# Stick-breaking stage: the gate's Exp and Ln one projection piece later, its product behind the taps, and the diagonal mask as an fp32r product

## The chip, the cores and the metric

One core of a Trainium2 chip runs the whole program in one launch. The metric is the device time of one execution in microseconds (us). The engines are named as the profile names them: PE (matrix engine), PEld (its weight loads), DVE (vector), ACT (scalar), POOL (GpSimd) and SP (the engine that issues most DMAs).

## The reference

A sequence of 1024 tokens with 1024 features goes through two blocks. The first (a gated MLP with spatial mixing, then a dilated window attention) is not touched. The second block projects each token and mixes with three groups of heads. These parts of it matter here:

```python
def stick_breaking_attention(q, k, v, valid):
    ...
        z = jnp.einsum('bhqd,bhkd->bhqk', q[:, :, start:end], k[:, :, :end]).astype(jnp.float32) * scale
        mask = (pos[None, :end] < pos[start:end, None]) & valid[None, :end]
        log_keep = jnp.where(mask, jax.nn.log_sigmoid(-z), 0.0)
        csum = jnp.cumsum(log_keep, axis=-1)
        log_w = jax.nn.log_sigmoid(z) + (csum[..., -1:] - csum)
        w = jnp.where(mask, jnp.exp(jnp.where(mask, log_w, 0.0)), 0.0)
    ...
    xbc = jax.nn.silu(causal_depthwise_conv(jnp.concatenate([xs, bm, cm], axis=-1) * vmask, conv_w, conv_b))
    ...
    y = y.reshape(bsz, L, SSD_W) * jax.nn.silu(z.astype(f32))
```

A query sees only the keys before it, so the blocks on the diagonal of the score matrix are masked. The projection's units xs, bm and cm go through a convolution of four taps and a silu; the units z, q and g of the other groups go through a silu alone. The kernel computes silu(y) as y * exp(-ln(1 + exp(-y))).

## The kernel before, in words

The stage is `projection_and_sticks` (L2492). It runs from about 2050 to 2600 us of the execution. Several things are interleaved in it by hand, and each engine follows the order that `drive` (L2585) writes out.

*The projection.* 27 units of 128 output features are computed for 1040 tokens. Each unit u has three pieces (j = 0, 1, 2: 352, 344 and 344 tokens). On PE a piece is 24 products of fp32r operands (L155: for each of 8 groups of features, three combinations of upper and lower halves). The weights of a unit are split beforehand into an upper half by ACT (L137, called by `w.split_hi` in piece j = 1 of the unit before) and a lower half by DVE (L142, `w.split_lo`, also in piece j = 1). DVE evicts each piece with a multiplication (`evict`, L2996) once PE has finished it. SP loads the weights two units ahead.

*The gates.* Units 7 to 14 go through the convolution (`is_x`), units 15 to 22 through the silu alone (`is_silu`). For a convolution unit v, DVE runs taps 0 and 1 in piece (v+1, 0) (L3074, L3076), and taps 2 and 3 (L3080, two instructions) and a clamp into the tile `ce` (L3083) in piece (v+1, 1). For a silu unit it runs a clamp alone in piece (v+1, 1) (L3089). ACT runs Exp (L2742) in piece (v+1, 1), then Ln (L2745) and Exp (L2747) in piece (v+1, 2), all on `ce`. DVE multiplies in piece (v+2, 0) (`finish`, L3011), and SP stores the unit in piece (v+2, 1).

*The sticks.* There are 56 slots (4 heads by 14 blocks of 128 keys with up to 512 queries). In slot c PE computes the scores of slot c+1 (L2918, fp32 operands), on the diagonal adds the mask by a product of the identity with a constant of 0 and -1e30 (L2921, fp32 operands), then adds the running sums to the scores of slot c (L2931: two products with a matrix of -1, where earlier blocks exist; L2933: two products with a triangle of -1), then runs the values of slot c-1 (L2902), then a share of a piece. ACT runs Abs, Exp and Ln (L2767, L2769, L2771) on the scores of c+1, the Exp of slot c (L2777), and the upper halves of the accumulator and of the sticks (L2780, L2786). DVE runs the accumulator (L3101, L3103), the softplus (L3112), and the lower halves (L3117, L3121). PE writes the next scores into a bank only once L2777 has read it, and waits before L2931 and L2933 for the lower halves.

*The state-space chunks.* Behind the sticks, phases of the chunked recurrence (class `Ssd`, L2274) take the place of the slots. Among them, L2342 on PE reads `ab`, which DVE copies in L2409; L2387 on ACT reads what the transposes of L2348 wrote, and PE's L2354 overwrites that bank.

Pieces 15 to 59 lie in the slots, at most one ends in a slot; the later ones lie between the phases. On each engine the instructions of a slot or phase stand ahead of those of its piece, and a waiting instruction holds up all behind it. All synchronisation is by semaphores. The constants come from `constants` (L3978); ACT copies the triangle and the matrix of -1 into fp32r tiles at the stage's start (L2711, L2712).

Of the kernel before, what the change touches and what calls it, by code (L numbers as in the profile page):

```python
# [16 lines left out]
F32R = mybir.dt.float32r  # L17
ACT = mybir.ActivationFunctionType
# [3 lines left out]
P = 128  # L22
# [4 lines left out]
HALF = 512  # L27
# [2457 lines left out]
def stick_tiles(nc):  # L2485

    with Stage(nc, "hs") as st:
        heads = st.sb("heads", [P, 4, LM])
        return heads, (st.sb("acc_lo", [P, HALF], F32R), st.sb("tri", [P, P], F32R), st.sb("ones", [P, P], F32R))


def projection_and_sticks(nc, a, w, hi, lo, inv, x, x_again, x_out, over_x, heads, hg, keep, table, cst, proj, conv, o_cat, ident, ones):  # L2492
# [10 lines left out]
    NU = len(units)  # L2503
# [16 lines left out]
    k_groups = lambda c: range(KT * rest * c // N, KT * rest * (c + 1) // N) if 0 <= c < N else ()  # L2520
    in_slot = lambda c: [first_slot + x // KT for x in k_groups(c) if x % KT == KT - 1]
    tok = lambda kt: (0, META) if kt == 0 else (META + (kt - 1) * P, P)
    neg_tri, neg_ones, neg, blocks = (cst[n] for n in ("neg_suffix", "neg_ones", "not_before", "block64"))
    with Stage(nc, "pr") as st:
        heads, (acc_lo, tri_r, ones_r) = heads
        qn, kn = ([heads[:, 2 * b + i, :] for i in range(2)] for b in range(2))
        vt, rows, sd_tile, sticks = over_x
        dtf, tmp, af = (rows[n] for n in ("dtf", "tmp", "af"))
# [166 lines left out]
        def _(act):  # L2695
# [13 lines left out]
            act.wait_ge(s_par, 16 * 7)  # L2709
            act.wait_ge(s_table, 16)  # L2710
            nc.scalar.activation(tri_r[:, :], neg_tri, ACT.Copy)  # L2711
            nc.scalar.activation(ones_r[:, :], neg_ones, ACT.Copy).then_inc(s_tri, 1)  # L2712
            for u in (2,):
                w.split_hi(act, u % 2, u // 2, free=(s_mm, 3 * (u - 2) + 3))
# [6 lines left out]
            def piece(p):  # L2721
                u, j = p // 3, p % 3
                if j == 0 and u - 3 in qk:
                    root(u - 3)
                if j == 1 and u + 1 < NU:
                    w.split_hi(act, (u + 1) % 2, (u + 1) // 2, free=(s_mm, 3 * (u - 1) + 3))
                if u - 2 in qk:
                    i = qk.index(u - 2)
                    if j == 0:
                        act.wait_ge(s_ev, 3 * (u - 2) + 3)  # L2730
                        wait(act, s_blk, 3 * i)
                        nc.scalar.activation(ce[:, :], ev[(u - 2) % 3][:, TAPS - 1:], ACT.Square).then_inc(s_psq, 1)
                    c0, c1 = PIECES[j]
                    act.wait_ge(s_blk, 3 * i + j + 1)
                    if j == 0:
                        wait(act, s_nrm, i - 1)
                    nc.scalar.activation(cy[i % 2][:, c0:c1], pb[:, 0:c1 - c0], ACT.Ln, bias=eps[:, :], scale=1.0 / HD).then_inc(s_pb, 1)
                if gated(u - 1):
                    n = n_gated(u - 1)
                    if j == 1:  # L2740
                        act.wait_ge(s_cm, n + 1)
                        nc.scalar.activation(ce[:, :], ce[:, :], ACT.Exp, scale=-1.0).then_inc(s_cx, 1)  # L2742
                    if j == 2:
                        act.wait_ge(s_cx, n + 1)
                        nc.scalar.activation(ce[:, :], ce[:, :], ACT.Ln, bias=1.0).then_inc(s_cl, 1)  # L2745
                        act.wait_ge(s_cl, n + 1)
                        nc.scalar.activation(ce[:, :], ce[:, :], ACT.Exp, scale=-1.0).then_inc(s_ce, 1)  # L2747
                if (u, j) == (DT + 2, 0):
                    act.wait_ge(s_sdp, 64)
                    nc.scalar.activation(par[:, 2:3], par[:, 1:2], ACT.Exp).then_inc(s_dte, 1)  # L2750
                    act.wait_ge(s_dt, 2)
                    nc.scalar.activation(tmp, tmp, ACT.Exp, scale=-1.0).then_inc(s_dte, 1)
                    act.wait_ge(s_dte, 2)
                    nc.scalar.activation(tmp, tmp, ACT.Ln, bias=1.0).then_inc(s_dte, 1)
                if (u, j) == (DT + 4, 0):
                    act.wait_ge(s_dtc, 5)
                    for name in ("ecum", "wend", "elast"):
                        nc.scalar.activation(keep[name], keep["cum" if name == "ecum" else name], ACT.Exp).then_inc(s_dtx, 1)
# [75 lines left out]
        def _(pe):  # L2834
# [71 lines left out]
            def slot(c):  # L2906
                if c + 1 < N:
                    h, (qb, kt, q0, n, diag) = (c + 1) // NS, steps[(c + 1) % NS]
                    hs = slice((h % 2) * HD, (h % 2 + 1) * HD)
                    k0, mp = tok(kt)  # L2910
                    b = (c + 1) % 2
                    if (c + 1) % NS == 0:
                        pe.wait_ge(s_nrm, 2 * (h // 2) + 2)
                    if c < 1:
                        pe.wait_ge(s_ev, 6)
                        pe.wait_ge(s_tri, 1)
                    wait(pe, s_w, c)
                    last = nc.tensor.matmul(zb[b][0:mp, 0:n], kn[h // 2][hs, k0:k0 + mp], qn[h // 2][hs, META + q0:META + q0 + n],  # L2918
                                            start=True, stop=False, skip_group_check=True)
                    if diag:  # L2920
                        last = nc.tensor.matmul(zb[b][0:mp, 0:P], ident, neg, start=False, stop=False, skip_group_check=True)  # L2921
                    last.then_inc(s_z, 1)
                if 0 <= c < N:
                    qb, kt, q0, n, diag = steps[c % NS]
# [26 lines left out]
        def _(dve):  # L2951
# [60 lines left out]

            def piece(p):
                u, j = p // 3, p % 3
                if j == 1 and u + 1 < NU:
                    w.split_lo(dve, (u + 1) % 2, (u + 1) // 2)
                if j == 0 and u - 3 in qk:
                    i = qk.index(u - 3)
                    dve.wait_ge(s_scaled, 1)
# [2 lines left out]
                                                   cy[i % 2][:, :], ALU.mult, ALU.mult).then_inc(s_nrm, 1)  # L3022
                    dve.wait_ge(s_nrm, i + 1)
                evict(u, j)
                if (u, j) == (DT + 1, 1):
                    dve.wait_ge(s_kept, 16 * KT)
                    dve.wait_ge(s_sdp, 64)
                    dve.wait_ge(s_ev, 3 * u)
                    nc.vector.memset(dtf[:, 0:P - META], 0.0)
                    nc.vector.memset(tmp[:, 0:P - META], 0.0)  # L3030
                    nc.vector.tensor_scalar(dtf[:, P - META:], ev[DT % 3][0:SSD_HEADS, TAPS - 1:], par[:, 0:1], None, ALU.add).then_inc(s_dt, 1)
                    dve.wait_ge(s_dt, 1)
                    nc.vector.scalar_tensor_tensor(tmp[:, P - META:], dtf[:, P - META:], -1.0, dtf[:, P - META:], ALU.mult, ALU.max).then_inc(s_dt, 1)
# [17 lines left out]
                if u - 2 in vs:  # L3051
# [10 lines left out]
                            nc.vector.tensor_copy(vt[i][:, 4:8, :], src).then_inc(s_pb, 1)  # L3062
                    else:
                        nc.vector.tensor_copy(vt[i][:, 8, :], pb[:, 0:P]).then_inc(s_pb, 1)
                if j == 0 and gated(u - 2):
                    finish(u - 2)
                if is_x(u - 1):
                    v, n = u - 1, n_gated(u - 1)
                    src = ev[v % 3]
# [7 lines left out]
                    if j == 1:  # L3077
# [3 lines left out]
                        dve.wait_ge(s_cc, 4 * n + 4)  # L3081
                        wait(dve, s_out, n)
                        nc.vector.tensor_scalar(ce[:, :], y, LOWEST, None, ALU.max).then_inc(s_cm, 1)  # L3083
                if is_silu(u - 1) and j == 1:
                    v, n = u - 1, n_gated(u - 1)
                    wait(dve, s_gone[v % 2], 16 * (n // 2))
# [891 lines left out]
def constants():  # L3978
# [3 lines left out]
        "ones": (i >= 0) & (j >= 0),  # L3982
        "neg_suffix": np.where(i >= j, -1, 0),
        "neg_ones": np.full((P, P), -1),
        "not_before": np.where(i < j, 0, -1e30),
        "block64": i // 64 == j // 64,
        "upto": i <= j,
        "levels": np.concatenate([(i // B == j // B) & (i % B < B // 2) & (j % B >= B // 2)
# [161 lines left out]
```

## Time and profile before

| what | us |
| --- | --- |
| median of three runs | 3622.37 |
| lowest and highest run | 3618.87, 3626.86 |
| the profiled execution, its own time | 3614.36 |
| its span in the trace | 3612.6 |
| PE busy in the span | 3451.5 (96%) |
| DVE busy | 2170.2 (60%) |
| ACT busy | 1537.2 (43%) |
| mean granted clock of PE, share of full speed | 0.978 |

Times in a row are microseconds from the start of the span. A row of the order of time gives start, duration, engine, line, operation, output and inputs, their shapes, the count of merged instructions, and in brackets how long the engine was idle before it and what ended that. A matmul's duration includes its passage through the array; how fast PE moves on is seen from the start of the next row. PEclk is the granted clock as a share of 2.4 GHz.

### The profile page before, as it was taken

What the parts mean: (1) busy time and instruction counts of PE and PEld (TensorE: products, weight loads), DVE (VectorE), ACT (ScalarE), POOL (GpSimd) and SP (SyncE); (2) the same over time, 40 slices, a digit from 0 to 9 for tenths busy, and PEclk for the clock granted to TensorE, in tenths of its full rate; (3) what the DMA queues carried; (4) which work ended last, traced back from release to release, by engine and by line L of the source; (5) the groups of instructions that cost most, each with busy time, mean ns of one, the idle gap of its engine ahead of it and who ended that gap; (6) DMA issues with size and microseconds to landing.
All of it is one profiled execution on the core that took longest, in us unless ns stands there. A gap on an engine that the chain in (4) does not pass through costs nothing. (4 is left out here: it accounts for less than half of the span.)

```text
span 3612.6 us, 48153 instructions
## 1 busy us (share of the span) xinstructions
PE 3451.5 (96%) x17578; PEld 2817.6 (78%) x17578; DVE 2170.2 (60%) x4264; ACT 1537.2 (43%) x3062; POOL 121.9 (3%) x151
## 2 busy tenths in 40 slices
PE   8999999989999999999999799999879989999999
PEld 6878887867777777777777687778867877878887
DVE  5477773575555666666675646656666566644443
ACT  4254453445444454544444445555224322232222
POOL 0000001000000000000000200000000000000000
PEclk9999999999999999999999999999989999999999
DMA  4232225622111221222233300112232222322223
GB/s 147 94 106 92 88 91 187 193 68 62 59 59 55 65 66 63 68 65 64 67 100 123 124 28 32 50 56 77 96 108 91 96 86 72 108 93 94 99 94 123
DMA packets 162585, 316.84 MB, mean 88 GB/s; under 512 B 33744, under 2 KB 79360, under 8 KB 162224
## 3 DMA queue, kind: packets, MB, share of 16 engines
q1 hardware_dynamic: 144432, 268.49, 22.5%
q0 software_dynamic: 15808, 36.89, 3.3%
q10 hardware_dynamic: 2112, 8.39, 0.6%
q8 instruction: 142, 2.33, 0.3%
q14 instruction: 91, 0.75, 0.1%
HBM read 260.22 MB, written 59.71 MB: 89 GB/s over the span
## 5 line engine op out<-in xcount | busy, mean ns | idle before, releaser
L142 DVE TENSOR_TENSOR all_w_lo<-all_w_raw,all_w_hi 128x1024 fp32r<-128x1024 f32 x241 | 295.1, 1225 | 256.8 <-ACT all_w_hi L137 256.8
L137 ACT ACTIVATE all_w_hi<-all_w_raw 128x1024 fp32r<-128x1024 f32 x241 | 253.5, 1053 | 454.8 <-PE om_z L155 261.5
L155 PE MATMUL om_z<-all_hi,all_w_hi 128*128 128x512 f32 x640 | 256.9, 401 | 7.5 <-DVE all_w_lo L142 4.3
L155 PE MATMUL om_z<-all_hi,all_w_lo 128*128 128x512 f32 x640 | 255.1, 399 | 0.0
L155 PE MATMUL om_z<-all_lo,all_w_hi 128*128 128x512 f32 x640 | 253.6, 396 | 0.0
L2122 DVE CUSTOM_DVE_ANT_0 at_logit<-da_qk,at_bias 128x256 f32<-128x256 f32 (+1 forms) x384 | 130.1, 377 | 164.2 <-issue 163.6
L155 PE MATMUL pr_g<-all_hi,all_w_hi 128*128 128x344 f32 (+1 forms) x624 | 217.7, 349 | 11.4 <-PEq L45 4.9
L1668 ACT ACTIVATE at_p<-at_logit,da_pair_max 128x256 f32<-128x256 f32 (+1 forms) x384 | 177.5, 465 | 100.3 <-DVE da_pair_max L2122 100.3
L1660 ACT ACTIVATE at_pt<-da_tr 128x512 f32<-128x512 f32 (+1 forms) x192 | 101.2, 527 | 263.6 <-PE da_tr L1860 263.4
L155 PE MATMUL pr_g<-all_hi,all_w_lo 128*128 128x344 f32 (+1 forms) x624 | 206.4, 331 | 0.0
L155 PE MATMUL pr_g<-all_lo,all_w_hi 128*128 128x344 f32 (+1 forms) x624 | 205.2, 329 | 0.0
L155 PE MATMUL om_z<-om_h_hi,all_w_hi 128*128 128x512 f32 x512 | 202.3, 395 | 1.7 <-DVE all_w_lo L142 1.7
L155 PE MATMUL om_z<-om_h_lo,all_w_hi 128*128 128x512 f32 x512 | 200.1, 391 | 0.0
L155 PE MATMUL om_z<-om_h_hi,all_w_lo 128*128 128x512 f32 x512 | 200.0, 391 | 0.0
L3968 DVE TENSOR_TENSOR all_yo<-all_yo,om_z 128x512 f32<-128x512 f32 x80 | 55.0, 687 | 183.4 <-PE om_z L155 183.3
L1870 PE MATMUL da_pv<-at_v,at_pt 128*128 128x64 f32 x1280 | 164.1, 267 | 0.0
L1870 PEld LDWEIGHTS da_pv<-at_v,at_pt 128*128 128x128 f32 x1280 | 159.8, 192 | 1.9
L2139 DVE TENSOR_TENSOR da_o<-da_pv,da_rden 128x128 f32<-128x128 f32 x192 | 56.0, 292 | 167.4 <-PE da_pv L1870 161.8
L155 PEld LDWEIGHTS om_z<-all_hi,all_w_hi 128*128 128x128 f32 x640 | 121.9, 190 | 36.9 <-DVE all_w_lo L142 4.5
L1196 ACT ACTIVATE all_w_hi<-all_w_raw 128x512 fp32r<-128x512 f32 x190 | 118.3, 623 | 72.4 <-PE da_by L1214 23.8
L3863 ACT ACTIVATE om_h_hi<-om_m 128x512 fp32r<-128x512 f32 x64 | 40.4, 632 | 254.5 <-DVE om_m L3966 254.5
L155 PEld LDWEIGHTS om_z<-all_lo,all_w_hi 128*128 128x128 f32 x640 | 121.6, 190 | 27.8
(827 smaller groups left out, 8908.0 us busy)
## 6 DMA issues: line engine op xcount, KB each, us to landing
all_w_raw<-in_w_mlp SPq DMA_DIRECT2D x128, 512.0 KB, 3.4
all_w_raw<-in_w_qkv SPq DMA_DIRECT2D x136, 256.0 KB, 2.7
all_w_raw<-in_w_ug SPq DMA_DIRECT2D x48, 512.0 KB, 4.1
all_w_raw<-in_w_in SPq DMA_DIRECT2D x27, 512.0 KB, 3.5
all_w_raw<-in_w_v SPq DMA_DIRECT2D x20, 512.0 KB, 4.6
vhat<-ag_vst ACTq DMA_DIRECT2D x4, 2048.0 KB, 7.4
ow_v<-vhat SPq DMA_DIRECT2D x16, 512.0 KB, 3.4
da_before<-o_groups POOLq DMA_DIRECT2D x32, 256.0 KB, 3.9
```

The source lines that it names most:

```text
L137: self.nc.scalar.activation(self.hi[b][:, :], self.raw[b][:, :], ACT.Copy).then_inc(self.hi_done[b], 1)
L142: self.nc.vector.tensor_tensor(self.lo[b][:, :], self.raw[b][:, :], self.hi[b][:, :].bitcast(F32), ALU.subtract).then_inc(self.lo_done[b], 1)
L155: last = self.nc.tensor.matmul(out, wp[b][:, w], ap[:, k, cols], start=(k == 0 and m == 0), stop=(k == KT - 1 and m == 2))
L1196: self.nc.scalar.activation(self.hi[n % self.slots], self.tile[name], ACT.Copy, scale=self.scales[j] if name in ("a11", "a12") else 1.0).t ...
L1660: nc.scalar.activation(pt[t % 2][:, 0:wd], tr[:, 0:wd], ACT.Copy).then_inc(s_pt, 1)
L1668: last = nc.scalar.activation(p[t % 2][:, hh, 0:wd], logit[t % 2][:, hh, 0:wd], ACT.Exp, scale=-1.0, bias=pair_max[:, t, hh:hh + 1], accum ...
L1870: last = nc.tensor.matmul(pv[:, 64 * hh:64 * hh + 64], pt[t % 2][:, i * P:i * P + P], v[:, t + x, 64 * hh:64 * hh + 64], start=(x == 0), s ...
L2122: last = nc.vector.tensor_tensor_reduce(out=logit[t % 2][:, hh, 0:wd], in0=qk[hh][:, 0:wd], in1=bias[ag][hh][x][:, :], scale=1.0, scalar=3 ...
L2139: nc.vector.tensor_tensor(o[:, t, :].rearrange("p (h c) -> p h c", h=2), pv[:, 0:P].rearrange("p (h c) -> p h c", h=2), rden[:, t, :].rear ...
L3863: nc.scalar.activation(h_hi[:, i, :], m[n % 2][:, :], ACT.Square)
L3968: nc.vector.tensor_tensor(x[:, i, halves[h]], x[:, i, halves[h]], z[b][:, :], ALU.add).then_inc(s_ev, 1)
```

## The change

- ACT runs the gate's Exp and Ln together in piece (v+1, 2), and the last Exp in piece (v+2, 0).
- DVE evicts a piece ahead of splitting the lower half of the next weights, and runs `finish` of unit v behind taps 0 and 1 of unit v+1.
- The mask of the diagonal blocks is the product of the fp32r triangle, which was already there, with a new constant `edge` in one more fp32r tile. `edge` has 2^100 in its last row and -2^100 just above the diagonal; under the triangle of -1 the two cancel for a key before the query, and give -2^100 otherwise.

```diff
--- before.py
+++ after.py
@@ -2486,7 +2486,7 @@
 
     with Stage(nc, "hs") as st:
         heads = st.sb("heads", [P, 4, LM])
-        return heads, (st.sb("acc_lo", [P, HALF], F32R), st.sb("tri", [P, P], F32R), st.sb("ones", [P, P], F32R))
+        return heads, (st.sb("acc_lo", [P, HALF], F32R), *(st.sb(n, [P, P], F32R) for n in ("tri", "ones", "edge")))
 
 
 def projection_and_sticks(nc, a, w, hi, lo, inv, x, x_again, x_out, over_x, heads, hg, keep, table, cst, proj, conv, o_cat, ident, ones):
@@ -2520,9 +2520,9 @@
     k_groups = lambda c: range(KT * rest * c // N, KT * rest * (c + 1) // N) if 0 <= c < N else ()
     in_slot = lambda c: [first_slot + x // KT for x in k_groups(c) if x % KT == KT - 1]
     tok = lambda kt: (0, META) if kt == 0 else (META + (kt - 1) * P, P)
-    neg_tri, neg_ones, neg, blocks = (cst[n] for n in ("neg_suffix", "neg_ones", "not_before", "block64"))
+    neg_tri, neg_ones, edge, blocks = (cst[n] for n in ("neg_suffix", "neg_ones", "edge", "block64"))
     with Stage(nc, "pr") as st:
-        heads, (acc_lo, tri_r, ones_r) = heads
+        heads, (acc_lo, tri_r, ones_r, edge_r) = heads
         qn, kn = ([heads[:, 2 * b + i, :] for i in range(2)] for b in range(2))
         vt, rows, sd_tile, sticks = over_x
         dtf, tmp, af = (rows[n] for n in ("dtf", "tmp", "af"))
@@ -2709,6 +2709,7 @@
             act.wait_ge(s_par, 16 * 7)
             act.wait_ge(s_table, 16)
             nc.scalar.activation(tri_r[:, :], neg_tri, ACT.Copy)
+            nc.scalar.activation(edge_r[:, :], edge, ACT.Copy)
             nc.scalar.activation(ones_r[:, :], neg_ones, ACT.Copy).then_inc(s_tri, 1)
             for u in (2,):
                 w.split_hi(act, u % 2, u // 2, free=(s_mm, 3 * (u - 2) + 3))
@@ -2735,16 +2736,16 @@
                     if j == 0:
                         wait(act, s_nrm, i - 1)
                     nc.scalar.activation(cy[i % 2][:, c0:c1], pb[:, 0:c1 - c0], ACT.Ln, bias=eps[:, :], scale=1.0 / HD).then_inc(s_pb, 1)
-                if gated(u - 1):
+                if gated(u - 1) and j == 2:
                     n = n_gated(u - 1)
-                    if j == 1:
-                        act.wait_ge(s_cm, n + 1)
-                        nc.scalar.activation(ce[:, :], ce[:, :], ACT.Exp, scale=-1.0).then_inc(s_cx, 1)
-                    if j == 2:
-                        act.wait_ge(s_cx, n + 1)
-                        nc.scalar.activation(ce[:, :], ce[:, :], ACT.Ln, bias=1.0).then_inc(s_cl, 1)
-                        act.wait_ge(s_cl, n + 1)
-                        nc.scalar.activation(ce[:, :], ce[:, :], ACT.Exp, scale=-1.0).then_inc(s_ce, 1)
+                    act.wait_ge(s_cm, n + 1)
+                    nc.scalar.activation(ce[:, :], ce[:, :], ACT.Exp, scale=-1.0).then_inc(s_cx, 1)
+                    act.wait_ge(s_cx, n + 1)
+                    nc.scalar.activation(ce[:, :], ce[:, :], ACT.Ln, bias=1.0).then_inc(s_cl, 1)
+                if gated(u - 2) and j == 0:
+                    n = n_gated(u - 2)
+                    act.wait_ge(s_cl, n + 1)
+                    nc.scalar.activation(ce[:, :], ce[:, :], ACT.Exp, scale=-1.0).then_inc(s_ce, 1)
                 if (u, j) == (DT + 2, 0):
                     act.wait_ge(s_sdp, 64)
                     nc.scalar.activation(par[:, 2:3], par[:, 1:2], ACT.Exp).then_inc(s_dte, 1)
@@ -2918,7 +2919,7 @@
                     last = nc.tensor.matmul(zb[b][0:mp, 0:n], kn[h // 2][hs, k0:k0 + mp], qn[h // 2][hs, META + q0:META + q0 + n],
                                             start=True, stop=False, skip_group_check=True)
                     if diag:
-                        last = nc.tensor.matmul(zb[b][0:mp, 0:P], ident, neg, start=False, stop=False, skip_group_check=True)
+                        last = nc.tensor.matmul(zb[b][0:mp, 0:P], tri_r[:, :], edge_r[:, :], start=False, stop=False, skip_group_check=True)
                     last.then_inc(s_z, 1)
                 if 0 <= c < N:
                     qb, kt, q0, n, diag = steps[c % NS]
@@ -3012,8 +3013,6 @@
 
             def piece(p):
                 u, j = p // 3, p % 3
-                if j == 1 and u + 1 < NU:
-                    w.split_lo(dve, (u + 1) % 2, (u + 1) // 2)
                 if j == 0 and u - 3 in qk:
                     i = qk.index(u - 3)
                     dve.wait_ge(s_scaled, 1)
@@ -3022,6 +3021,8 @@
                                                    cy[i % 2][:, :], ALU.mult, ALU.mult).then_inc(s_nrm, 1)
                     dve.wait_ge(s_nrm, i + 1)
                 evict(u, j)
+                if j == 1 and u + 1 < NU:
+                    w.split_lo(dve, (u + 1) % 2, (u + 1) // 2)
                 if (u, j) == (DT + 1, 1):
                     dve.wait_ge(s_kept, 16 * KT)
                     dve.wait_ge(s_sdp, 64)
@@ -3062,8 +3063,6 @@
                             nc.vector.tensor_copy(vt[i][:, 4:8, :], src).then_inc(s_pb, 1)
                     else:
                         nc.vector.tensor_copy(vt[i][:, 8, :], pb[:, 0:P]).then_inc(s_pb, 1)
-                if j == 0 and gated(u - 2):
-                    finish(u - 2)
                 if is_x(u - 1):
                     v, n = u - 1, n_gated(u - 1)
                     src = ev[v % 3]
@@ -3081,6 +3080,8 @@
                         dve.wait_ge(s_cc, 4 * n + 4)
                         wait(dve, s_out, n)
                         nc.vector.tensor_scalar(ce[:, :], y, LOWEST, None, ALU.max).then_inc(s_cm, 1)
+                if j == 0 and gated(u - 2):
+                    finish(u - 2)
                 if is_silu(u - 1) and j == 1:
                     v, n = u - 1, n_gated(u - 1)
                     wait(dve, s_gone[v % 2], 16 * (n // 2))
@@ -3982,7 +3983,7 @@
         "ones": (i >= 0) & (j >= 0),
         "neg_suffix": np.where(i >= j, -1, 0),
         "neg_ones": np.full((P, P), -1),
-        "not_before": np.where(i < j, 0, -1e30),
+        "edge": 2.0 ** 100 * ((i == P - 1).astype(int) - (i == j - 1)),
         "block64": i // 64 == j // 64,
         "upto": i <= j,
         "levels": np.concatenate([(i // B == j // B) & (i % B < B // 2) & (j % B >= B // 2)
```

## Rows read from the trace of the kernel before

**Rows 1.** Windows: engines' busy us (instructions), PE's granted clock, DMA share, GB/s.

```profile
2100.00:2200.00 100.00, 96.76 (x540) 79.82 (x539) 54.38 (x101) 53.96 (x105) 0.00 (x0) 0.98 0.09 28
2200.00:2300.00 100.00, 90.15 (x481) 74.02 (x480) 65.36 (x115) 58.35 (x111) 0.00 (x0) 0.91 0.12 40
2300.00:2400.00 100.00, 89.82 (x462) 72.62 (x461) 64.99 (x108) 54.98 (x101) 0.00 (x0) 0.91 0.12 41
```

**Rows 2.** PE's waits, 2100 to 2440: us in total, times, longest.

```profile
PE pr_zb L2918 <- ACT pr_wt L2777: 17.4, 9, 3.7
PE pr_zb L2931 <- DVE ox_sticks L3121: 4.6, 6, 1.5
```

**Rows 3.** The longest waits, same stretch, all engines: one of ACT.

```profile
ACT pr_ce L2742 <- DVE pr_ce L3083: 43.9, 8, 7.5
```

**Rows 4.** Order of time around one stalled slot of the sticks.

```profile
2249.06 1.04 ACT L137 ACTIVATE all_w_hi<-all_w_raw 128x1024 fp32r<-128x1024 f32 x1
...
2249.19 0.69 DVE L3121 TENSOR_TENSOR ox_sticks<-pr_sp,pr_sp_hi 128x512 fp32r<-128x512 f32 x1
...
2249.59 1.12 PE L2918 MATMUL pr_zb<-hs_heads 64*128 64x512 f32 x2
2250.13 1.23 DVE L142 TENSOR_TENSOR all_w_lo<-all_w_raw,all_w_hi 128x1024 fp32r<-128x1024 f32 x1 [0.25 <-ACT all_w_hi L137]
...
2250.64 0.45 PE L2931 MATMUL pr_zb<-ox_sticks,hs_ones 128*128 128x384 f32 x1
...
2251.27 0.51 DVE L2996 TENSOR_TENSOR pr_ev<-pr_g,all_inv 128x344 f32<-128x344 f32 x1
...
2251.70 2.63 DVE L3080 SCALAR_TENSOR_TENSOR pr_cy<-pr_ev,pr_taps,pr_cy 128x1040 f32<-128x1040 f32 x2
...
2254.36 0.70 DVE L3083 TENSOR_SCALAR pr_ce<-pr_cy 128x1040 f32<-128x1040 f32 x1
...
2255.10 1.07 ACT L2742 ACTIVATE pr_ce<-pr_ce 128x1040 f32<-128x1040 f32 x1 [5.00 <-DVE pr_ce L3083]
2255.12 0.55 DVE L3103 TENSOR_TENSOR pr_acc<-pr_acc,pr_sp 128x384 f32<-128x384 f32 x1
...
2258.43 0.69 DVE L3112 SCALAR_TENSOR_TENSOR pr_sp<-pr_zb,pr_e 128x512 f32<-128x512 f32 x1 [2.76 <-ACT pr_e L2771]
...
2258.94 2.07 PE L2918 MATMUL pr_zb<-hs_heads 64*128 64x512 f32 x2 [3.67 <-ACT pr_wt L2777]
...
2260.04 0.69 DVE L3121 TENSOR_TENSOR ox_sticks<-pr_sp,pr_sp_hi 128x512 fp32r<-128x512 f32 x1
```

**Rows 5.** Windows of 5 us, columns as in rows 1.

```profile
2280.00:2285.00 5.00, 2.33 (x9) 1.04 (x8) 2.59 (x4) 4.79 (x10) 0.00 (x0) 1.00 0.00 0
2525.00:2530.00 5.00, 5.00 (x24) 4.97 (x24) 2.26 (x5) 0.83 (x1) 0.00 (x0) 0.70 0.00 0
```

**Rows 6.** Order of time around two stalls in the state-space phases.

```profile
2485.48 0.52 DVE L2996 TENSOR_TENSOR pr_ev<-pr_g,all_inv 128x344 f32<-128x344 f32 x1 [1.21 <-PE pr_g L155]
...
2488.28 1.91 PE L2342 MATMUL pr_ob<-mixers_cst,ox_ab 128*128 128x128 f32 x15 [2.17 <-DVE ox_ab L2409]
...
2519.93 1.22 DVE L142 TENSOR_TENSOR all_w_lo<-all_w_raw,all_w_hi 128x1024 fp32r<-128x1024 f32 x1 [2.69 <-ACT all_w_hi L137]
...
2523.19 0.58 ACT L2387 ACTIVATE pr_sp<-pr_zb 128x512 f32<-128x512 f32 x1
...
2523.83 0.66 PE L2354 MATMUL pr_zb<-all_ident,ox_zf 128*128 128x128 f32 x4 [3.51 <-ACT pr_sp L2387]
```

**Rows 7.** Order of time on PE in one diagonal slot.

```profile
2196.44 0.49 PE L2921 MATMUL pr_zb<-mixers_cst,all_ident 128*128 128x128 f32 x2
...
2196.68 0.31 PE L2933 MATMUL pr_zb<-pr_sp_hi,hs_tri 128*128 128x128 f32 x1
...
2196.82 0.28 PE L2933 MATMUL pr_zb<-ox_sticks,hs_tri 128*128 128x128 f32 x1
```

**Rows 8.** Order of time on ACT near the stage's start.

```profile
2061.37 0.29 ACT L2711 ACTIVATE hs_tri<-mixers_cst 128x128 fp32r<-128x128 f32 x1
```


## The prediction, made before the change was run

> **What bounds the kernel now.** I first read the windows [rows 1], because the change lives in one stage, the second block's projection with the stick-breaking attention in it, from about 2050 to 2600 us. While no gated unit is in it (2100 to 2200) PE is busy 96.76 of 100 us at a granted clock of 0.98. In the next two hundreds it is busy 90.15 and 89.82 us at 0.91. So PE paces the stage, and from 2200 on it loses in two ways: 20 us stand idle, and the busy time is partly at the lower of the clock's two levels, 1.2 instead of 2.4 GHz. At half speed a busy share of 1 - 0.91 in windows with 180 busy us costs 180 x 0.09 = 16.2 us.
>
> Then the list of PE's waits [rows 2]: 17.4 us in 9 waits stand before L2918 (the next slot's scores), which waits for ACT's L2777 (the Exp that makes the attention weights); 4.6 us in 6 waits stand before L2931, which waits for DVE's L3121. The full list says why ACT is late [rows 3]: it stood 43.9 us in 8 waits at L2742, the gate's first Exp, for DVE's L3083, the clamp behind the taps of the convolution.
>
> One such wait in order of time [rows 4] is the case to follow. ACT has split the next weights by 2250.10 and stands at L2742 for 5.00 us: DVE must first split the lower half (L142), evict (L2996), run two taps (L3080) and clamp (L3083), to about 2255.0. Queued behind L2742 on ACT are the next slot's Abs, Exp, Ln and L2777. They finish after 2258.4, so PE, which had ended its work at 2258.94 - 3.67 = 2255.27, stands 3.67 us. Then its L2918 takes 2.07 us where it took 1.12 at 2249.59: the clock has fallen. Windows of 5 us show which stalls do that [rows 5]: from 2280 to 2285 PE is busy 2.33 of 5 us, idle in two stalls of under 2 us, and the clock stays 1.00; behind the stall of 3.51 us [rows 6] it is 0.70. Among the stalls here those of 1.5 us mostly pass, and those above 2 us mostly don't.
>
> **The gate on ACT.** Removed: ACT's wait at piece j = 1. Exp and Ln stand together at j = 2, where the clamp has long been done, since at most one piece falls in a slot; the last Exp stands at the next j = 0. ACT's work per unit is as before (three activations of 1.07 us); j = 2 keeps two, j = 0 takes the one that j = 1 gives up. In that case [rows 4] ACT is then free at 2250.10, its three small activations and L2777 follow the scores that are ready at 2250.64, and L2918 of the next slot finds its weights made. The 17.4 us go, as cause. What is late next is DVE, which still has the clamp ahead of the next slot's chain.
>
> **The order on DVE.** The eviction now comes ahead of L142. In the same case: eviction at 2249.88 (behind the previous L3121), L142 at 2250.31, taps at 2251.45, clamp at 2254.11, accumulator (L3103) at 2254.73, L3112 at about 2255.20. From L3112's start to L3121's end the trace shows 2260.73 - 2258.43 = 2.30 us with ACT's upper half between [rows 4]. So the sticks are ready at 2257.5, and PE wants them at 2255.27 + 1.05 (the scores, 2249.59 to 2250.64) = 2256.3. A stall of 1.2 us is left before L2931, where 3.67 stood. I worked the other seven convolution units in the same way, from their own shapes: 1.35, 0, 0.45, 1.05, 0.2, 0 and 1.1 us; the small ones are slots with short diagonal blocks. All eight: 5.3 us. Three of these hold up to 1.2 us from the swap itself: where L142 used to run while DVE waited for PE's piece, it now stands behind the eviction. For the gates without taps the clamp follows at once and no new stall comes.
>
> Of the 4.6 us before L2931, three waits of 2.0 us together come in the slot right behind one that ACT made late, and belong to the 5.3 now; 2.6 stay (bounds: none or all of the 4.6). Idle saved among the sticks: 17.4 + 2.0 - 5.3 = 14.1 us. The last product (L3011) behind the taps delays only its store; DVE waits there for an Exp that ACT has run before the eviction. SP's stores of the finished units go out about 2.1 us later (the two taps of piece j = 0 now stand ahead of L3011: half of L3080's two a piece), and so do POOL's loads that follow the last of them, whose data PE takes several phases later: nothing; without that cover it would cost 2.1 us twice.
>
> **The clock.** With stalls of 1.35 us at most I expect most of the 16.2 us back, and keep 3.5 for one or two falls: 12.7 us. Bounds: 6 us, if the stalls of 1.0 to 1.5 us fall together with others, and 16.2.
>
> **The diagonal mask.** 32 products (64 records: two for each fp32 product) become fp32r products of one record. At full clock the fp32 one moves PE on by 0.24 us (2196.44 to 2196.68 [rows 7]), an fp32r one of the same 128x128 shape with the same weights by 0.14 (to 2196.82). Saved: 32 x 0.10 = 3.2 us; a little of it lies in slots where DVE ends the wait, so I take 2.9. Bounds: 0 (PE gets no further by it) and 32 x 0.24 = 7.7 (the product costs nothing). The Trainium skill ("FP8 and Floating Point Precision", TensorE Precision Notes) says that true FP32 makes four passes through the array; by that alone the product would fall to a quarter, 0.06 us, and the sum would be 2.6 us better. No quarter is seen here: the trace has 0.14 us against 0.24 [rows 7], and the measurement decides. The copy of the new constant is one ACT instruction of 0.29 us [rows 8], ahead of the split of unit 2, whose DVE half stands behind five evictions: hidden; with that cover gone it costs 0.3.
>
> **Behind the sticks.** Two stalls of the state-space phases are touched [rows 6]. At 2523.83 PE had stood 3.51 us for ACT's L2387, which was queued behind L2742, since ACT had finished its split before L142 started at 2519.93. PE's own transposes, which L2387 reads, were done when its stall began, 2523.83 - 3.51 = 2520.3. Without the wait L2387 starts then instead of at 2523.19: 2.9 us, and the clock's fall behind it (0.70 over 5 us [rows 5]) another 1.5. Against it, at 2485.48 DVE had done L142 while it waited for PE; now L142 stands behind the eviction and ahead of L2409, for which PE already stands 2.17 us: 1.2 us lost. Net 3.2 us.
>
> **Sum.** 14.1 + 12.7 + 2.9 + 3.2 = 32.9 us. The profiled execution took 3614.36 (span 3612.6 and 1.8 around it): 3581.5. It lies 8.0 below the median of the runs, 3622.37, so against the median the change gives 3589.5; I say 3590. Nothing behind the stage is changed, and it moves forward as a whole: its last stretch is a DVE chain that starts from PE's phases.
>
> **Rivals.**
> *DVE takes the wait over (17%).* The swap and the taps hit all twelve gated units among the sticks, not eight: 1.2 us is left at each, 14.4 of 19.4, the clock gives back half (8), the mask 3, the phases 1. Gain 17 us: 3605. For it: DVE was already the releaser of 4.6 us, and its slots get shorter when PE is faster. Against it: gates without taps need 2 us less of DVE.
> *The stall only changes its name (5%).* PE waits as long before L2931 as it did before L2918, the clock falls as often, and the mask alone is left: 3 us, 3619. The order of time [rows 4] speaks against it: the chain from the clamp to the sticks is 2.8 us and starts at the same time as before, but no longer has ACT's Exp of 1.07 and four activations in front.
> *Slower (3%).* The swap's place is L142 between eviction and taps. If the upper halves were ready long before PE's piece ends, each of twelve slots would have 1.2 us more on DVE, 14.6 in all, on top of unchanged stalls, less 3 for the mask: 3634. It decides once ACT's L137 ends over 1.2 us ahead of the piece; in the case above it ends 0.4 us behind it (2250.10 against the end at about 2249.6), and only at 2483.05 is DVE that early.
> *The mask saves nothing* lies inside the forecast: 3593.
>
> **How the numbers follow.** The forecast has 75%. Its own range is 3577 to 3600: no stalls left and the whole clock back is 9 us better, a few us are the scatter of medians (the three runs span 8 us), and on the other side the clock's lower bound. To hold eight in ten with the first rival partly in, the range is 3577 to 3610. A measurement of this kernel tells about 0.2%, 7 us, from no change. Faster (under 3615): 0.75 + 0.17 less 0.01 = 0.91; within: 0.06; slower: 0.03.
>
> **What would show it.** Right: no wait of PE on L2777 between 2196 and 2416 except crumbs; ACT's waits at the gate's Exp for L3083 gone; waits before L2931 for L3121 between 5 and 11 us in all, none above 1.5; the granted clock of these two hundreds at 0.97 or more; the mask's product one record of 128x128 and PE moving on within 0.15 us. The stall before L2354 under 1 us, that before L2342 near 3.4. Wrong: L3121 as releaser of 15 us or more, the clock still near 0.91, or PE waiting for lower halves (L142).

## The result, and the profile after

The changed kernel takes 3584.19 us (median of 4 runs, 3583.30 to 3586.79); the kernel before takes 3624.61 us beside it (4 runs, 3618.87 to 3630.26). The ratio is 0.989 with a 95% interval of 0.9872 to 0.9907: 40 us, or 1.1%, faster. The forecast was 3590, with 3577 to 3610 as its range.

The windows of the middle of the stage, of the kernel after, answer to [rows 1]:

```profile
2100.00:2200.00 100.00, 96.64 (x528) 79.50 (x527) 52.78 (x100) 55.25 (x109) 0.00 (x0) 0.97 0.08 26
2200.00:2300.00 100.00, 97.22 (x558) 79.39 (x557) 78.30 (x137) 68.19 (x127) 0.00 (x0) 1.00 0.13 48
2300.00:2400.00 100.00, 97.51 (x556) 80.29 (x555) 72.07 (x126) 66.74 (x125) 1.85 (x2) 1.00 0.21 68
```

Where gated units run, PE was busy 90 of 100 us at a clock of 0.91; now it is busy 97 at 1.00. The number of its instructions per window rises from 481 to 558: this is the gain. Its waits from 2100 to 2420 us, kernel after, answer to [rows 2]:

```profile
PE pr_zb L2932 <- DVE ox_sticks L3122: 5.2, 5, 1.4
PE pr_pb L2885 <- ACT pr_ce L2733: 2.2, 1, 2.2
PE pr_zb L2934 <- DVE ox_sticks L3122: 1.2, 1, 1.2
```

The 17.4 us before the scores are gone altogether. (Lines have moved: L2932 is L2931 of before, L2934 is L2933, L3122 is L3121, L2919 is L2918, L2922 is L2921, L2778 is L2777, L2997 is L2996, L2885 is L2884, and L3079 and L3082 are L3080 and L3083.) What is left of the sticks' own waits is for their lower half, 5.2 us before L2932 and 1.2 before L2934. The 2.2 us before L2885 were 2.2 in the kernel before too. The slot that the prediction followed [rows 4] looks like this in the order of time, kernel after:

```profile
2243.09 0.51 DVE L2997 TENSOR_TENSOR pr_ev<-pr_g,all_inv 128x344 f32<-128x344 f32 x1
...
2243.51 1.22 DVE L142 TENSOR_TENSOR all_w_lo<-all_w_raw,all_w_hi 128x1024 fp32r<-128x1024 f32 x1
...
2244.65 2.63 DVE L3079 SCALAR_TENSOR_TENSOR pr_cy<-pr_ev,pr_taps,pr_cy 128x1040 f32<-128x1040 f32 x2
...
2245.93 0.59 ACT L2778 ACTIVATE pr_wt<-pr_zb 128x512 f32<-128x512 f32 x1
...
2247.32 0.70 DVE L3082 TENSOR_SCALAR pr_ce<-pr_cy 128x1040 f32<-128x1040 f32 x1
...
2248.54 1.12 PE L2919 MATMUL pr_zb<-hs_heads 64*128 64x512 f32 x2
...
2249.79 1.05 ACT L2742 ACTIVATE pr_ce<-pr_ce 128x1040 f32<-128x1040 f32 x1
2249.93 0.69 DVE L3122 TENSOR_TENSOR ox_sticks<-pr_sp,pr_sp_hi 128x512 fp32r<-128x512 f32 x1
...
2250.67 0.51 PE L2932 MATMUL pr_zb<-ox_sticks,hs_ones 128*128 128x512 f32 x1 [1.01 <-DVE ox_sticks L3122]
```

ACT makes the weights at 2245.93, before DVE even starts the clamp at 2247.32, so PE starts the next scores at 2248.54 without a wait and at full clock (1.12 us, not 2.07). ACT's Exp of the gate (L2742) follows at 2249.79, behind the slot's own work, and no longer waits for the clamp. DVE is late next, by 1.01 us; the prediction had 1.2.

The two stalls behind the sticks, kernel after, in order of time, answer to [rows 6]:

```profile
2451.66 0.52 DVE L2997 TENSOR_TENSOR pr_ev<-pr_g,all_inv 128x344 f32<-128x344 f32 x1 [2.35 <-PE pr_g L155]
...
2452.09 1.22 DVE L142 TENSOR_TENSOR all_w_lo<-all_w_raw,all_w_hi 128x1024 fp32r<-128x1024 f32 x1
...
2455.47 2.83 PE L2342 MATMUL pr_ob<-mixers_cst,ox_ab 128*128 128x128 f32 x12 [3.18 <-DVE ox_ab L2409]
...
2489.28 0.60 ACT L2387 ACTIVATE pr_sp<-pr_zb 128x512 f32<-128x512 f32 x1 [0.46 <-PE pr_zb L2348]
...
2489.93 0.66 PE L2354 MATMUL pr_zb<-all_ident,ox_zf 128*128 128x128 f32 x4 [0.69 <-ACT pr_sp L2387]
```

L2354 waits 0.69 instead of 3.51 us. L2342 waits 3.18 instead of 2.17 us, since DVE, which stood idle for 2.35 us ahead of the eviction, has the split of 1.22 us still to do behind it. And the mask, on PE, kernel after, answers to [rows 7]:

```profile
2115.51 0.33 PE L2922 MATMUL pr_zb<-hs_edge,hs_tri 128*128 128x128 f32 x1
2115.68 0.28 PE L2932 MATMUL pr_zb<-ox_sticks,hs_ones 128*128 128x128 f32 x1
```

One record, and PE moves on after 0.17 us instead of 0.24. The median over the 32 products is 0.164 instead of 0.244 us, so that together they save 2.6 us.

To compare kernels I use two windows of each: from the first to the last scores (the sticks), and from there to the last eviction (behind). What I call the clock's part is the length of a stretch times one minus its granted clock. With the two digits that the windows below show it would be good to 1.8 us only, so I add it up over windows of 5 us, which is good to 0.2. It counts a little too much where PE stands idle at the low clock. Kernel before, then kernel after:

```profile
2106.30:2464.30 358.00, 332.83 (x1788) 271.50 (x1788) 222.06 (x393) 211.94 (x398) 1.84 (x2) 0.95 0.12 42
2464.30:2597.90 133.60, 123.39 (x803) 118.88 (x801) 91.12 (x158) 49.57 (x88) 7.93 (x11) 0.99 0.27 92
```

```profile
2107.00:2430.50 323.50, 314.87 (x1757) 256.75 (x1756) 221.49 (x393) 213.53 (x398) 1.85 (x2) 0.99 0.14 46
2430.50:2562.70 132.20, 123.64 (x803) 119.16 (x801) 90.26 (x159) 49.72 (x88) 7.94 (x11) 0.99 0.27 93
```

The sticks are 34.5 us shorter: idle time 25.2 to 8.6 us (16.5 less), the clock's part 19.0 to 3.4 us (15.6 less), and 2.4 us less work, which agrees with the 2.6 of the mask. Behind them 1.4 us are gained, with a clock's part of 1.7 us in both.

### The profile page after: what moved, and what is told of

It reads as the page before. It is cut to its first block and busy times, and to the rows that moved or that the text cites. A ratio compares the mean times of both kernels' runs of the same rounds, so it can differ in the third digit from the quotient of the medians.

```text
span 3582.6 us, 48090 instructions
## 1 busy us (share of the span) xinstructions
PE 3441.7 (96%) x17546; PEld 2808.9 (78%) x17546; DVE 2168.3 (61%) x4264; ACT 1539.0 (43%) x3063; POOL 122.0 (3%) x151
```

## The experiments

The kernel before ran beside each, with medians of 3622 to 3625 us. Idle time and the clock's part of all of them stand in a table at the end.

### ACT's order alone

The kernel before, with this one edit:

```diff
-                if gated(u - 1):
-                    n = n_gated(u - 1)
-                    if j == 1:
+                if gated(u - 1) and j == 2:
...
+                if gated(u - 2) and j == 0:
```

> Before, with ACT's order alone changed (Exp and Ln at j = 2, last Exp at the next j = 0); DVE's order and the mask as before. My theory: the cause is the one wait of ACT for the clamp, so nearly all of the gain is here: 35 to 39 us below before, PE's waits on L2777 gone, at most 6 us of waits on L3121, granted clock 0.98 or more from 2200 to 2400. Rival (the parts need each other: with finish still ahead of the taps, DVE now stands at each j = 0 for an Exp that ACT runs in the same piece, and the taps start later): at most 25 us, with DVE's wait at L3011 for L2747 of 0.5 us or more in each of 16 units.

Measured: 3583.14 us, ratio 0.9887 (0.9869 to 0.9905). The windows of the sticks and behind them, of this kernel:

```profile
2108.40:2434.90 326.50, 318.36 (x1788) 260.20 (x1788) 222.01 (x393) 213.67 (x398) 1.85 (x2) 0.99 0.14 46
2434.90:2564.10 129.20, 122.01 (x803) 117.46 (x801) 90.32 (x158) 49.82 (x88) 7.95 (x11) 1.00 0.28 95
```

One moved wait carries the whole gain. The sticks are 3.0 us longer than in the changed kernel with the same clock's part (3.4 us): that is the mask. The stretch behind them is 3.0 us shorter, 1.3 us by the swap and 1.7 us by a fall of the clock that this execution does not have. The waits for the lower halves are 5.9 us, within the 6 expected. The rival (the parts need each other) is out.

### The mask alone

The kernel before, with the mask's product and its constant as in the change.

> Before, with the mask alone as an fp32r product. My theory: 32 products that move PE on 0.14 instead of 0.24 us: 3 us below before, between 0 and 5. Rival (the mask lies on the path from the scores to ACT, so that the stalls on L2777 and the clock's falls shrink too): 8 us or more.

Measured: 3627.69 us, ratio 1.0007 (0.9994 to 1.002): nothing that can be told. The rival of 8 us is out; my 3 us are not seen either. The profile shows where they went (window of the sticks, this kernel):

```profile
2107.30:2470.40 363.10, 337.73 (x1757) 276.38 (x1756) 222.28 (x393) 211.87 (x398) 1.85 (x2) 0.92 0.12 41
```

Idle time is 25.4 us as before, but the clock's part is 29.1 us instead of 19.0: nearly the same stalls cost 10 us more in this execution. It is not this execution alone. Over its 12 runs the granted clock of the whole execution is 0.9735 in the mean, over the 23 of the kernel before 0.9754; that is some 7 us of clock, while the mean time is 3.8 us longer, so that about 3 us are gained outside the clock. Why the clock is lower here no run shows.

### DVE's two moves alone

The kernel before, with `evict` ahead of `split_lo` and `finish` behind the taps.

> Before, with DVE's two moves alone (eviction ahead of the lower split, finish behind the first taps); ACT and mask as before. My theory: the clamp that ACT waits for comes up to 1.2 us later in three of eight units, the rest is hidden: 0 to 4 us above before. Rival (the earlier eviction, or taps that start before finish, relieve PE): 5 us or more below before.

Measured: 3631.41 us, ratio 1.0017 (1.0005 to 1.0028): 6 us above before by the ratio, interval 2 to 10. PE's waits behind the sticks, this kernel:

```profile
PE pr_ob L2342 <- DVE ox_ab L2409: 3.7, 2, 3.2
PE pr_zb L2354 <- ACT pr_sp L2387: 3.5, 1, 3.5
```

The stall before L2342 has grown to 3.2 us, that of L2354 has not moved. Among the sticks PE stands idle for 25.4 us (before 25.2), and the clock's part is 29.1 us. Without the clock's part the stretch behind them is 133.0 us, against 131.9 before. So these moves give nothing and cost a little. I had expected 0 to 4 us. The mean granted clock of its 12 runs, 0.9747 against 0.9754, accounts for some 2.5 of the 6 us; for the rest beyond the 1.1 us behind the sticks no run shows the cause.

### The change without the swap

```diff
+                if j == 1 and u + 1 < NU:
+                    w.split_lo(dve, (u + 1) % 2, (u + 1) // 2)
                 if j == 0 and u - 3 in qk:
...
                 evict(u, j)
-                if j == 1 and u + 1 < NU:
-                    w.split_lo(dve, (u + 1) % 2, (u + 1) // 2)
```

> The changed kernel with the lower split put back ahead of the eviction. My theory: the swap costs up to 1.2 us in three slots and at L2342: 2 to 4 us faster than the changed kernel, and PE's wait before L2342 near 2.0 instead of 3.18 us. Rival (the swap is part of the gain, since a split that waits for ACT's upper half no longer holds up the eviction): 2 us or more slower than the changed kernel.

Measured: 3583.21 us (3573.19 to 3592.59), ratio 0.9886 (0.9866 to 0.9907); the changed kernel had 0.989. The time can't tell the 2 to 4 us. The trace can: behind the sticks 129.2 us instead of 132.2, and PE's first wait before L2342 is 2.2 instead of 3.2 us. This kernel, behind the sticks:

```profile
2433.60:2562.80 129.20, 121.99 (x803) 117.51 (x801) 90.25 (x158) 49.83 (x88) 7.95 (x11) 1.00 0.28 95
```

Of the 3.0 us, 1.7 are a fall of the clock that the changed kernel has behind the grown stall and this execution has not; 1.3 us are the swap itself. Among the sticks this kernel is 1.0 us longer, all of it the clock's (5.1 against 3.4 us), and the whole stage is 502.5 against 503.0 us.

### The change with finish ahead of the taps

> The changed kernel with finish (L3011) put back ahead of the first taps. My theory: finish is off the path, since nothing of the slots waits for its place among DVE's work of piece j = 0: the same as the changed kernel within 2 us, idle of PE among the sticks 8.6 +- 1 us, stage 503 +- 1 us without the clock. Rival (finish behind the taps is what hides the Exp that now stands in the same piece): PE's waits on L3121 2 us or more higher, 3 us or more slower.

Measured: 3588.94 us (3578.60 to 3589.80), ratio 0.9897 (0.988 to 0.9913). The median is 4.8 us above the changed kernel's, where I had expected 2 at most, but the two intervals overlap. The trace decides: idle time of PE among the sticks is 8.6 us and its waits on L3122 are 5.2 us in 5, as in the changed kernel; the stage is 502.7 against 503.0 us. `finish` is off the path, as expected. Behind the sticks this execution shows something else (this kernel):

```profile
2430.00:2560.50 130.50, 121.93 (x803) 117.47 (x801) 90.27 (x159) 49.71 (x88) 7.92 (x11) 1.00 0.28 94
```

PE waits 3.2 us before L2342, as in the changed kernel, and here the clock does not fall behind it: 130.5 instead of 132.2 us.

### The change with the old mask

> The changed kernel with the mask put back to fp32. My theory: without stalls the mask's 3 us lie open on PE: busy time without the clock's part 3 us higher among the sticks, 2 to 4 us slower in all. Rival (it lies beside the waits for L3121 and gives nothing): within 1 us, idle of PE lower by as much.

Measured: 3586.55 us, ratio 0.99 (0.9884 to 0.9916). Among the sticks (this kernel):

```profile
2105.20:2429.90 324.70, 317.08 (x1788) 259.24 (x1788) 221.48 (x393) 213.62 (x398) 1.84 (x2) 0.99 0.14 46
```

The sticks are only 1.2 us longer than in the changed kernel, but the clock's part is 1.7 us against 3.4. Without it they take 323.0 against 320.1 us: the old mask costs 2.9 us. Idle time is 7.6 against 8.6 us, and the waits for the lower halves are 5.4 against 6.4: that 1.0 us the new mask gives back, as the rival said, and it is already in the 2.9. The median is 2.4 us above the changed kernel's, which the time alone could not tell.

### The lower split in the idle piece

The changed kernel, to better it:

```diff
+                if j == 2 and u + 1 < NU:
+                    w.split_lo(dve, (u + 1) % 2, (u + 1) // 2)
                 if j == 0 and u - 3 in qk:
...
                 evict(u, j)
-                if j == 1 and u + 1 < NU:
-                    w.split_lo(dve, (u + 1) % 2, (u + 1) // 2)
```

> The changed kernel with the lower split moved to piece j = 2, ahead of the eviction there, so that taps and clamp follow the eviction at once in j = 1. My theory: the 5.2 us of waits before the sticks' sums hang on DVE's load of 5 us in j = 1; with 1.2 us less of it they fall to about 2, that before L2342 from 3.2 to 2.2 or less: 4 to 7 us faster than the changed kernel. Rival (the split now ends too late for the first piece of the next unit): new waits of PE before L155 for L142, 1 us or more in each of some 20 units, 10 us or more slower.

Measured: 3622.79 us, ratio 0.9997 (0.9987 to 1.0006): the whole gain is lost. PE's waits over the stage and one of them in order of time, this kernel:

```profile
PE pr_g L155 <- DVE all_w_lo L142: 26.2, 14, 4.3
...
PE pr_zb L2932 <- DVE ox_sticks L3122: 0.4, 1, 0.4
```

```profile
2252.98 0.31 PE L155 MATMUL pr_g<-all_lo,all_w_hi 128*128 128x344 f32 x1
...
2256.33 1.22 DVE L142 TENSOR_TENSOR all_w_lo<-all_w_raw,all_w_hi 128x1024 fp32r<-128x1024 f32 x1
...
2257.60 0.43 PE L155 MATMUL pr_g<-all_hi,all_w_hi 128*128 128x352 f32 x1 [4.31 <-DVE all_w_lo L142]
```

My part came true: the waits before the sticks' sums fell from 5.2 to 0.4 us. The rival's did too: a slot's share of PE is 6.4 of a piece's 8 groups, so in the slot in which piece 2 ends the first groups of the next unit begin, and they need the lower half at once. It is done 4.3 us too late, behind the slot's own chain on DVE. I had assumed a slot of slack there, and there was none. The waits are 14 and not some 20.

### ACT made late again

The changed kernel, with a dose of work where the wait had stood:

```diff
...
+                if gated(u - 1) and j == 1:
+                    act.wait_ge(s_zout, 48)
+                    for _ in range(14):
+                        wait(act, s_dose, len(doses))
+                        nc.scalar.activation(zero[:, :], ones[:, 0:P - META], ACT.Copy).then_inc(s_dose, 1)
+                        doses.append(1)
```

> The changed kernel with 14 short chained activations (112 columns, some 0.3 us each, 4 us in all) on ACT in piece j = 1 of each of the 16 gated units, where the wait for the clamp stood; no data depend on them. My theory: it is ACT's lateness alone that stalls PE. ACT's waits there were 5 us plus the Exp of 1.07, so 4 us bring back a part: waits before the scores for the weights' Exp of 3 to 12 us, clock falls with them, 8 to 25 us slower than the changed kernel. Rival (the gain came from the clamp and DVE's chain, and ACT has room in these slots): under 3 us slower.

Measured: 3602.76 us, ratio 0.9945 (0.9925 to 0.9965): 18.6 us above the changed kernel's median. One slot in order of time, this kernel (L2785 is the weights' Exp, L2926 the scores):

```profile
2241.49 4.56 ACT L2744 ACTIVATE pr_zero<-all_ones 128x112 f32<-128x112 f32 x14
...
2248.19 0.58 ACT L2785 ACTIVATE pr_wt<-pr_zb 128x512 f32<-128x512 f32 x1
...
2248.82 1.12 PE L2926 MATMUL pr_zb<-hs_heads 64*128 64x512 f32 x2 [2.02 <-ACT pr_wt L2785]
```

4.56 us of ACT bring back 2.02 us of PE's stall here, 5.5 us in 6 waits among the sticks and, behind them, the stall before L2354 (4.6 us). The waits for the lower halves before the sums grow too, from 5.2 to 7.0 us. DVE's program was not touched. ACT's lateness alone makes these stalls; a wait for work and work itself do the same.

### The stalls filled instead of removed

The kernel before, in PE's program, one slot behind the end of each piece j = 1 of a convolution unit:

```diff
+                if any(p % 3 == 1 and is_x(p // 3 - 1) for p in in_slot(c - 1)):
+                    for _ in range(16):
+                        nc.tensor.matmul(ob[0][:, HALF // 2:], tri_r[:, :], hi[:, 0, 0:HALF // 2], start=True, stop=True, skip_group_check=True)
```

The extra products write into the other half of a bank that holds values, and this kernel's output is not the reference's: it serves for its time alone. The work beside them is that of the kernel before.

> Before, with 16 extra fp32r products of 256 columns on PE (0.12 us each by the matmul rows, 1.9 us in all, results unused) in each of the eight places ahead of the scores for which PE waits for L2777. The work is as before, and the waits are filled instead of removed. My theory: the clock's fall is a cost of the idle time itself, 17 to 27 us of the stage; with the idle time filled to under 2 us per stall, waits on L2777 fall from 17.4 to 6 us or less, the clock's part to 8 us or less, and the kernel is 8 to 18 us faster than before although it does more. Rival (the clock falls whatever PE does in the wait, or it is the engine's mean load that matters): the same as before or slower, by up to 8 x 1.9 us where the fill does not fit.

Measured: 3619.02 us (11 runs), ratio 0.9983 (0.997 to 0.9996): 6 us faster than before, although PE does 128 products more. PE's waits and its window among the sticks, this kernel:

```profile
PE pr_zb L2931 <- DVE ox_sticks L3124: 4.5, 5, 1.4
PE pr_zb L2918 <- ACT pr_wt L2777: 4.5, 6, 1.8
```

```profile
2108.20:2462.80 354.60, 342.38 (x1917) 284.11 (x1916) 222.01 (x393) 212.15 (x398) 1.84 (x2) 0.97 0.13 42
```

Idle time is 12.2 instead of 25.2 us, and the clock's part 11.9 us; the kernels with 25 us idle had 19.0, 29.1 and 29.1. Over all 11 runs the granted clock of the whole execution is 0.9776 in the mean against 0.9751 beside it, some 9 us of clock for a time that is 6.0 us shorter in the mean. The direction is mine, since busy waiting gave time back; the size is not: I expected 8 to 18 us and a clock's part of 8 at most.

### ACT's order and the mask, DVE as before

The kernel before, with the first and the third part of the change.

> Before, with ACT's order and the mask changed, DVE's order as before. My theory: the mask's 2 to 3 us add to ACT's part, and the 3 us that the swap costs behind the sticks are saved: stage 500 +- 1.5 us, 3580 to 3584 us. Rival (without DVE's two moves something of the gain is missing): 3586 us or more.

Measured: 3583.16 us (3578.34 to 3588.71), ratio 0.9881 (0.9864 to 0.9898); stage 503.7 us, where I had expected 500 +- 1.5; of it 5.1 us are the clock's part among the sticks. Behind the sticks it takes 130.8 us, 1.7 of them the clock's, so that 129.1 are left as in the other kernels without the swap (129.2). It ties with the changed kernel, with ACT's order alone and with the version without the swap. None of them beats the change by more than the scatter, and I can't say which is best.

## Why the prediction was right

**The bound and the cause.** Right, point by point: PE paces the stage, the 17.4 us hang on ACT's wait for the clamp, and moving that wait removes them. The kernel with ACT's order alone shows it from the one side, the dose on ACT from the other.

**What is late next.** Right: DVE, by the waits before the sticks' sums. I had 5.3 us left from the convolution units and 2.6 us of others, 7.9 in all; 5.2 us were measured before L2932, the followed slot 1.01 against 1.2. The idle term was 14.1 us forecast, 16.5 measured.

**The clock.** The mechanism is right, the size is the term that I had too small. In the pair of profiled executions the stage is 540.1 us before and 503.0 after. Of these 37.1 us the idle time gives 16.5 (forecast 14.1), the clock's part 15.6 (12.7), the work 2.4 (2.9), the stretch behind the sticks 1.4 (3.2), and 1.2 us lie ahead of the sticks, where nothing was changed. The two executions differ by 30.0 us only, not by 37.1, since outside the stage the one of the kernel before is 7.1 us shorter (3072.5 against 3079.6 us; the twelve profiled kernels span 3072.5 to 3083.2 there, with a mean of 3077.6). So about 5 of the 8.0 us by which it lay below the median were not the stage's. The clock of all runs is the better measure: 0.9754 in the mean of the 54 runs of the kernel before that ran beside the experiments, 0.9808 in the changed kernel's four, which makes some 19 us. I had 12.7 and 1.5. These 5 us of clock and 2.4 of idle time are the difference between the 32.9 us forecast and the 40 measured. The time itself was missed by 6 us and not by 8, since the kernel before was 2 us slower beside the changed one (3624.61) than in the three runs that I started from. The reading that stalls of 1.5 us mostly pass and those above 2 us mostly don't was loose as well: in the trace of the kernel before the clock is 0.71 from 2235 to 2240, behind a stall of 1.41 us, and 1.00 from 2488 to 2493, behind one of 2.17.

**The mask.** Forecast 0.14 us per product, measured 0.164, above the 0.15 that I had named as a sign; so a product saves 0.08 and not 0.10 us. Forecast 2.9 us of gain in all, measured 2.9 without the clock's part (the old mask put back), of which the rows explain 2.6. Alone in the kernel before it is hidden by the clock. The array's four passes for true FP32, of which the Trainium skill speaks ("FP8 and Floating Point Precision", TensorE Precision Notes), did not decide: 0.24 us became 0.17, not 0.06.

**Behind the sticks.** Forecast 3.2 us, measured 1.4. The stall before L2354 shrank as said (3.51 to 0.69), and the one before L2342 grew (2.17 to 3.18). Without the clock's part the stretch takes 131.9 us before, 129.2 with ACT's order alone and 130.5 with the swap too: 2.7 us gained (forecast 2.9) and 1.3 lost (forecast 1.2). What I left out is the clock behind the grown stall. In the changed kernel it is 0.66 there, over the 5 us of the next row, and this takes back the 1.5 us that I had counted for the fall behind L2354:

```profile
2455.00:2460.00 5.00, 4.53 (x23) 4.57 (x24) 2.43 (x6) 0.75 (x2) 0.00 (x0) 0.66 0.46 132
```

The execution with `finish` ahead of the taps had the same stall and no such fall (1.00, 130.5 us), so this loss comes and goes.

**The rivals.** DVE did not take the waits over, and the swap did not make it slower, though alone it did go the slower way. `finish` behind the taps is neutral.

## What to carry to other kernels

When an engine that serves two chains waits in program order for the slower one, look at what is queued behind the wait; moving the wait one step later, to where its data are long there, cost nothing here and gave 1.1%. Before moving a step into an engine's idle piece, find the first reader of its result in the other engine's program, not in the loop's index: there was no slot between them, and 40 us were at stake. When stalls bring the clock down, one profile gives a sample of the loss and not its size: take the granted clock from all runs.

## What the runs showed that I had not expected

Stalls of nearly the same length cost the clock very different amounts. The table gives the twelve profiled executions in us, the clock's part added up over windows of 5 us.

| kernel | idle among the sticks | clock's part there | sticks without it | behind the sticks | clock's part there | without it |
| --- | --- | --- | --- | --- | --- | --- |
| before | 25.2 | 19.0 | 339.0 | 133.6 | 1.7 | 131.9 |
| mask alone | 25.4 | 29.1 | 334.0 | 135.4 | 3.4 | 132.0 |
| DVE's moves alone | 25.4 | 29.1 | 337.6 | 136.4 | 3.4 | 133.0 |
| stalls filled | 12.2 | 11.9 | 342.7 | 133.7 | 1.7 | 132.0 |
| changed | 8.6 | 3.4 | 320.1 | 132.2 | 1.7 | 130.5 |
| finish first | 8.6 | 3.4 | 320.2 | 130.5 | 0.0 | 130.5 |
| old mask | 7.6 | 1.7 | 323.0 | 132.2 | 1.7 | 130.5 |
| ACT's order alone | 8.1 | 3.4 | 323.1 | 129.2 | 0.0 | 129.2 |
| without the swap | 8.1 | 5.1 | 319.4 | 129.2 | 0.0 | 129.2 |
| ACT's order and mask | 8.9 | 5.1 | 320.2 | 130.8 | 1.7 | 129.1 |
| dose on ACT | 16.1 | 6.8 | 328.4 | 137.3 | 3.4 | 133.9 |
| lower split in j = 2 | 30.1 | 13.7 | 343.2 | 130.8 | 1.7 | 129.1 |

With 25.2 to 25.4 us idle among the sticks the clock's part was 19.0 us in one execution and 29.1 in two others; with 7.6 to 8.9 us idle it was 1.7 to 5.1 in all six. But the sum of the idle time does not fix it: the dose on ACT, with 16.1 us idle, had less than the filled stalls with 12.2, and the lower split in j = 2, with the most idle time of all, had less than the kernel before. Their windows among the sticks, dose first:

```profile
2106.70:2441.90 335.20, 319.09 (x1757) 260.26 (x1756) 221.16 (x393) 255.33 (x552) 1.84 (x2) 0.98 0.14 45
2106.50:2463.40 356.90, 326.83 (x1757) 264.51 (x1756) 221.47 (x393) 214.11 (x398) 1.84 (x2) 0.96 0.13 43
```

What decides between them no run here shows. Filling half of the idle time with useless products made the kernel faster than leaving it empty, by 0.17%.
